# Two transformer blocks in one kernel: projections of the first block and the mixers moved from float32 matmuls to three passes of split operands

## What is computed

```python
h = rms_norm(x, gain)
proj = jnp.einsum('bsd,de->bse', h, w_in)   # q, k, v, g of three branches, q_idx, k_idx, w_idx, f_logit, merge_logit
oa = moba_attention(...) * silu(ga); ob = dsa_attention(...) * silu(gb); oc = forgetting_attention(...) * silu(gc)
y = einsum('nbsw,nwd->bsnd', stack([oa, ob, oc]), w_branch)
merged = jnp.sum(sigmoid(merge_logit).reshape(B, S, N_BRANCH, D_MODEL) * y, axis=2)
x = x + einsum('bsd,de->bse', merged, w_out)
```

```python
h = modulate(rms_norm_2(x, norm), shift, scale)
x = x + 0.5 * g * swiglu(h, w_in, w_out)                       # ffn1, ffn2
x = x + mod[5] * (concatenate([att, conv_or_na]) @ w_out)      # mixer, from pl = h @ w_in
```

## Time and profile before

| | us |
|---|---|
| median of 3 runs (2820.1 to 2823.27) | 2822.03 |
| the profiled execution, time | 2823.07 |
| its span | 2821.3 |
| TensorE matmuls busy | 2710.4 |
| VectorE / ScalarE / GpSimd busy | 1028.1 / 759.1 / 86.3 |
| DMA, mean | 125 GB/s |

### The profile page before, as it was taken

The page is one execution under the profiler, slowest core; times in us unless marked ns, Lnnn a source line. Parts: engine busy times, 40 slices in busy tenths (PEclk is TensorE's granted clock), DMA queues, the critical chain, the costliest instruction groups (busy, mean ns, idle before and its releaser), DMA issues.

```text
span 2821.3 us, 35941 instructions
## 1 busy us (share of the span) xinstructions
PE 2710.4 (96%) x14818; PEld 2130.8 (76%) x14818; DVE 1028.1 (36%) x1672; ACT 759.1 (27%) x1309; POOL 86.3 (3%) x97
## 2 busy tenths in 40 slices
PE   7999999999998999999999899999899999999899
PEld 6877788877886888874455478888688886766899
DVE  0142420142433433330475244333433342045654
ACT  1113311113314222223136242122422223135433
POOL 0000000000000000000380000000000000000000
PEclk9999999999999999999999999999999999999999
DMA  5334444334443232221255232223123222441453
GB/s 218 132 118 149 166 149 163 143 113 158 178 152 132 95 121 77 90 105 64 98 218 191 79 120 89 100 92 121 73 93 114 91 92 90 135 180 47 149 201 112
DMA packets 62656, 353.38 MB, mean 125 GB/s; under 512 B 14384, under 2 KB 17456, under 8 KB 26416
## 3 DMA queue, kind: packets, MB, share of 16 engines
q1 hardware_dynamic: 62512, 351.33, 35.1%
HBM read 350.26 MB, written 1.05 MB: 125 GB/s over the span
## 4 chain that ended last, share of the span: by engine, by line
PE 91%; DVE 5%; ACT 3%; issue 1%; DMA 1%; SPq 0%; ACTq 0%; DVEq 0%
PE psum L655 45%; PE psum L927 15%; PE psum L929 15%; PE psum L928 15%; DVE slab L1797 1%; PE psum L797 1%; ACT slab L1270 1%; DVE stat L1755 1%; DVE w_lo L1809 1%; ACT squares L1248 0%; DMA x<-in_x 0%; DVE squares L1682 0%; ACT slab L1290 0%; DVE psum L1751 0%; DVE slab L1768 0%
## 5 line engine op out<-in xcount | busy, mean ns | idle before, releaser
L655 PE MATMUL psum<-slab,wring 128*128 128x256 f32 (+1 forms) x3460 | 873.9, 413 | 7.0 <-ACT slab L1270 4.4
L655 PEld LDWEIGHTS psum<-slab,wring 128*128 128x128 f32 x3460 | 657.8, 192 | 202.8 <-issue 117.3
L927 PE MATMUL psum<-h_hi,w_hi 128*128 128x512 f32 (+1 forms) x1408 | 516.6, 367 | 21.3 <-DVE h_lo L1678 13.7
L928 PE MATMUL psum<-h_lo,w_hi 128*128 128x512 f32 (+1 forms) x1408 | 515.1, 366 | 0.0
L929 PE MATMUL psum<-h_hi,w_lo 128*128 128x512 f32 (+1 forms) x1408 | 514.9, 366 | 0.0
L1809 DVE TENSOR_TENSOR w_lo<-wring,w_hi 128x1024 fp32r<-128x1024 f32 (+1 forms) x240 | 317.8, 1330 | 330.1 <-ACT w_hi L1364 329.9
L1364 ACT ACTIVATE w_hi<-wring 128x1024 fp32r<-128x1024 f32 (+1 forms) x240 | 272.7, 1142 | 606.7 <-PE psum L929 534.7
L927 PEld LDWEIGHTS psum<-h_hi,w_hi 128*128 128x128 f32 x1408 | 269.1, 191 | 63.6 <-issue 19.2
L928 PEld LDWEIGHTS psum<-h_lo,w_hi 128*128 128x128 f32 x1408 | 269.2, 191 | 41.8
L929 PEld LDWEIGHTS psum<-h_hi,w_lo 128*128 128x128 f32 x1408 | 268.8, 191 | 41.8
L928 PE MATMUL psum<-hidden_lo,w_hi 128*128 128x512 f32 (+1 forms) x704 | 255.6, 363 | 0.0
(11 more groups left out here) (128 smaller groups left out, 1693.1 us busy)
## 6 DMA issues: line engine op xcount, KB each, us to landing
wring<-in_w_b_ffn_in SPq DMA_DIRECT2D x88, 1024.0 KB, 4.8
wring<-in_w_mod SPq DMA_DIRECT2D x72, 1024.0 KB, 4.8
wring<-in_w_b_ffn_out SPq DMA_DIRECT2D x64, 704.0 KB, 4.0
wring<-in_w_b_merge SPq DMA_DIRECT2D x24, 1024.0 KB, 4.8
wring<-in_w_b_out SPq DMA_DIRECT2D x16, 1024.0 KB, 4.8
wring<-in_w_b_in SPq DMA_DIRECT2D x16, 1024.0 KB, 4.9
wring<-in_w_b_q SPq DMA_DIRECT2D x12, 1024.0 KB, 4.8
wring<-in_w_b_k SPq DMA_DIRECT2D x12, 1024.0 KB, 4.8
```

What stands on the lines that cost most here:

```text
L655: return nc.tensor.matmul(out, lhsT, rhs, start=(k == 0), stop=(k == n - 1))
L927: nc.tensor.matmul(acc, wh[:, k, :], rhs_hi[k], start=(k == 0), stop=False)
L928: nc.tensor.matmul(acc, wh[:, k, :], rhs_lo[k], start=False, stop=False)
```

## The change

- All of q, k, v, g and merge of the first block, and b2.0.in, b2.0.out, b2.1.in, b2.1.out, run in three passes (`features3`, `tokens3`). qi, misc, branch and out of the first block, uq, ukv and the modulations stay float32.
- One sequence of weight pieces goes through the kernel (`piece_of`). Of a mixer chunk `w_hi` takes the rounded halves, and the differences are written into the ring slot, over the raw weights (`ring_lo`). A piece is rounded when the piece four before it is multiplied.
- Norms take their weight pieces `ahead`: two between the squares of k=6 and k=7, and two later, in place of the four ahead of all squares. b1 norms and mixer norms make `h_hi` and `h_lo` too. `ffn_weights` goes.
- Mixer outputs are written as hi and lo (a cast and a subtraction), and so is the convolution's (`split_conv`).
- Two modulation chunks move from the convolution to uq, and the convolution's mean, centre, square and variance two steps earlier. Buffers are laid out anew in two areas beside the FFN's parts. The one-hot rows give way to columns of the identity, and their DMA goes.

```diff
-MOD_PLACES = [("b1.0.att", 9), ("b1.1", 2), ("b1.1.att", 11), ("b2.0.n1", 2), ("b2.0.nm", 2), ("b2.0.conv", 5), ("b2.0.uq", 5), ("b2.0.heads", 6),
+MOD_PLACES = [("b1.0.att", 9), ("b1.1", 2), ("b1.1.att", 11), ("b2.0.n1", 2), ("b2.0.nm", 2), ("b2.0.conv", 3), ("b2.0.uq", 7), ("b2.0.heads", 6),
...
-        for at, kind in ((3, "mean"), (4, "center"), (5, "square"), (6, "var"), (12, "root"), (13, "scale"), (14, "silu")):
+        for at, kind in ((1, "mean"), (2, "center"), (3, "square"), (4, "var"), (12, "root"), (13, "scale"), (14, "silu")):
             out[at].append((kind, 0, 0))
+        for at, c in ((12, 0), (13, 1)):
+            out[at].append(("split", 0, c))
+    if nm.startswith("b1"):
+        for c in range(1, 12):
+            out[c].append(("split", l, c))
+    if nm == "b2.1.att":
+        for at, c in ((2, 0), (4, 1)):
+            out[at].append(("split", 1, c))
...
+def split_stage(s):
+
+    return ".ffn" in s or s in ("b2.0.in", "b2.0.out", "b2.1.in", "b2.1.out") or s[0:3] == "b1." and s[5:] in (
+        "merge",) + tuple(f"{part}{br}" for part in "qkvg" for br in range(3))
...
+            def features3(nm, c, rhs, N, tiles, first=0, rotating=None, close=True):
+
+                per = BANK // N
+                lo = mixer_lo(c)
+                for t in range(tiles):
+                    q = piece_of[c] + t
+                    if t % per == 0:
+                        label = f"{nm}.{first + t // per}"
+                        acc = take(label, rotating)
+                    out = acc[:, N * (t % per):N * (t % per) + N]
+
+                    pe.wait_ge(weights_split, q + 1)
+                    for k, (r_hi, r_lo, ready) in enumerate(rhs):
+                        if t == 0 and ready:
+                            if E.new(ready):
+                                pe.wait_ge(*E.at(ready))
+                        nc.tensor.matmul(out, mixer_hi(q)[:, k, :], r_hi, start=(k == 0), stop=False)
+                        nc.tensor.matmul(out, mixer_hi(q)[:, k, :], r_lo, start=False, stop=False)
+                        mm = nc.tensor.matmul(out, lo[:, k, P * t:P * t + P], r_hi, start=False, stop=(k == len(rhs) - 1))
+                    if t == tiles - 1 and close:
+                        E.name_next(f"w{c}")
+                    mm.then_inc(piece_multiplied, 1)
+                    E.step(piece_multiplied, label if t % per == per - 1 or t == tiles - 1 else None)
...
+            def tokens3(nm, c, lhs, halves, toks, first=0, close=True):
+
+                n = P * len(halves)
+                per = BANK // n
+                q = piece_of[c] + halves[0]
+                lo = mixer_lo(c)
+
+                pe.wait_ge(weights_split, piece_of[c] + halves[-1] + 1)
+                for i, t in enumerate(toks):
+                    if i % per == 0:
+                        label = f"{nm}.{first + i // per}"
+                        acc = take(label)
+                    out = acc[:, n * (i % per):n * (i % per) + n]
+                    out2 = out.rearrange("p (a n) -> p a n", n=P)
+                    last = close and i == len(toks) - 1
+                    for k, (l_hi, l_lo, ready) in enumerate(lhs):
+                        if ready:
+                            if E.new(ready):
+                                pe.wait_ge(*E.at(ready))
+                        hi = w_hi[:, q % PARTS:q % PARTS + len(halves), P * k:P * k + P]
+                        nc.tensor.matmul(out2, l_hi[:, P * t:P * t + P], hi, start=(k == 0), stop=False)
+                        mm = nc.tensor.matmul(out2, l_lo[:, P * t:P * t + P], hi, start=False, stop=False)
+                        if last and k == len(lhs) - 1 and len(halves) == 2:
+
+                            mm.then_inc(piece_multiplied, 1)
+                            E.step(piece_multiplied)
+                        mm = nc.tensor.matmul(out, l_hi[:, P * t:P * t + P], lo[:, k, P * halves[0]:P * halves[0] + n],
+                                              start=False, stop=(k == len(lhs) - 1))
+                    if last:
+                        E.name_next(f"w{c}")
+                        mm.then_inc(piece_multiplied, 1)
+                        E.step(piece_multiplied, label)
...
-            def norm(nm):
+            def norm(nm, ahead=None):
 
                 N = NORM_N[nm]
                 for k in range(KD):
+                    if k == KD - 1 and ahead:
+                        for i in range(2):
+                            ahead(i)
...
+            def round_piece(c, i):
+
+                q = piece_of[c] + i
+                act.wait_ge(landed[c % SLOTS], 16 * (c // SLOTS + 1))
+
+                if q >= PARTS:
+                    act.wait_ge(piece_multiplied, q - PARTS + 1)
+                A(mixer_hi(q), slot_of(c).rearrange("p (k n) -> p k n", n=256)[:, :, P * i:P * i + P], ACT.Copy).then_inc(weights_rounded, 1)
+
+            def round_chunk(c):
+                for i in range(2):
+                    round_piece(c, i)
...
-            def modulate(nm, l, which, N):
-
-
+            def modulate(nm, l, which, N, ahead):
+
+
+                if which != 1:
+                    for i in (2, 3):
+                        ahead(i)
                 if E.new(f"{nm}.mscale"):
                     act.wait_ge(*E.at(f"{nm}.mscale"))
                 for k in range(KD):
                     if E.new(f"{nm}.t{k}"):
                         act.wait_ge(*E.at(f"{nm}.t{k}"))
                     for g in range(N // SEQ):
-                        v = (h[:, k, :] if which == 1 else squares[:, k % 4, :])[:, SEQ * g:SEQ * g + SEQ]
-                        last = g == N // SEQ - 1
+                        v = squares[:, k % 4, SEQ * g:SEQ * g + SEQ]
                         A(v, v, ACT.Identity, scale=mscale[:, k, g:g + 1],
                           bias=mods[:, l, 24 * which + k, g:g + 1]).then_inc(shifted, 1)
-                        act.wait_ge(shifted, E.step(shifted, f"{nm}.h{k}" if last and which == 1 else None))
-                    if which != 1:
-                        A(h_hi[:, k, 0:N], squares[:, k % 4, 0:N], ACT.Copy).then_inc(shifted, 1)
-                        act.wait_ge(shifted, E.step(shifted, f"{nm}.hi{k}"))
+                        act.wait_ge(shifted, E.step(shifted))
+                    A(h_hi[:, k, 0:N], squares[:, k % 4, 0:N], ACT.Copy).then_inc(shifted, 1)
+                    act.wait_ge(shifted, E.step(shifted, f"{nm}.hi{k}"))
+                    if which == 1 and k == 3:
+                        for i in (2, 3):
+                            ahead(i)
+
+            def round_plain(nm, ahead):
+                for k in range(KD):
+                    if E.new(f"{nm}.t{k}"):
+                        act.wait_ge(*E.at(f"{nm}.t{k}"))
+                    A(h_hi[:, k, 0:SEQ], h_plain[:, k, :], ACT.Copy).then_inc(shifted, 1)
+                    act.wait_ge(shifted, E.step(shifted, f"{nm}.hi{k}"))
+                    if k == 3:
+                        for i in (2, 3):
+                            ahead(i)
...
+                            n = 8 * br + 2 * "qkvg".index(part) + j
+                            if n not in (14, 15, 23):
+                                round_chunk(flow[n + 2])
...
+                for n in (16, 17):
+                    round_chunk(flow[n])
...
+            def norm(nm, gain=None, to=None, ahead=None, early=True):
 
                 N = NORM_N[nm]
+                if ahead:
+                    for i in range(2):
+                        ahead(i)
...
+                for k in range(KD + 2):
+                    if ahead and k == (2 if early else 6):
+                        for i in (2, 3):
+                            ahead(i)
+                    if k >= 2 and ahead:
+
+                        plain = h_plain[:, k - 2, :] if gain is not None else squares[:, (k - 2) % 4, 0:N]
+                        if E.new(f"{nm}.hi{k - 2}"):
+                            dve.wait_ge(*E.at(f"{nm}.hi{k - 2}"))
+                        V.tensor_tensor(h_lo[:, k - 2, 0:N], plain, h_hi[:, k - 2, 0:N].bitcast(F32), ALU.subtract).then_inc(normed, 1)
+                        dve.wait_ge(normed, E.step(normed, f"{nm}.h{k - 2}"))
...
+            def split_piece(c, i):
+
+                q = piece_of[c] + i
+                raw = slot_of(c).rearrange("p (k n) -> p k n", n=256)[:, :, P * i:P * i + P]
+
+                dve.wait_ge(weights_rounded, q + 1)
+                V.tensor_tensor(mixer_lo(c)[:, :, P * i:P * i + P], raw, mixer_hi(q).bitcast(F32), ALU.subtract).then_inc(weights_split, 1)
+                E.step(weights_split)
+
+            def split_chunk(c):
+                for i in range(2):
+                    split_piece(c, i)
...
-                                V.tensor_copy(u["dst"], o).then_inc(probs_ready, 1)
+                                hi, lo = u["dst"]
+                                V.tensor_copy(hi, o).then_inc(probs_ready, 1)
+                                dve.wait_ge(probs_ready, E.step(probs_ready))
```

(38 more changed lines are left out.)

357 lines of the change are left out of this document (202 added, 155 removed).

## The result

| us | before | changed | ratio (95% interval) |
|---|---|---|---|
| median of four runs | 2822.52 | 2773.06 (2767.72 to 2774.93) | 0.9824 (0.981 to 0.9839) |
| span of the profiled execution | 2821.3 | 2773.1 | |
| mean granted clock of TensorE | 0.978 | 0.967 | |
| sum of TensorE's waits in its timeline | 102.1 | 169.4 | |

What follows compares the result with a forecast made beforehand. TensorE was taken as the bound, 91% of the chain of waits. From 2823.1 us, 132.2 saved on TensorE and 57.0 of longer waits added gave 2747.9, forecast 2748 us, with an 80% range of 2712 to 2785.

Steps and rivals of the forecast that it cites:

- rival 2: First block's attention: 22 steps with a split are paced by the splits, losing 1.3 us each, 29 us, 2777; chance 0.15.
- Gain on TensorE, 132.2: Converted projections: three passes save 97.0 us at N=256 and 38.7 at N=512, less 3.5 lost in b2.1.cv.
- Mix norms, +12 each: b2.0.nm and b2.1.nm: two roundings before the last square, then h_lo at 1.93 us a k; 24 us lost together.
- Norms of the first block, +7: b1.0 and b1.1: 2.0 us of rounding before the last square, then h_lo with two subtractions among them; 14 us lost together.
- Index products, +5.1: Each first-block layer: VectorE's splits of chunks 16 and 17 stand ahead of the RoPE TensorE waits for; 10.2 us lost together.
- Convolution -3, FFN norms -3.7: Second block: two modulation chunks fill the convolution wait; b2.0.n2 -6.3, b2.1.n1 -0.4, b2.0.n1 and b2.1.n2 +1.5 each.
- Behind it top-k shares VectorE with seven splits: hidden.: First block, behind the index products: top-k and splits take 2.0 + 2.4 us per 5.75 us; no loss charged.
- In the attentions of the first block ... nothing charged.: Steps of about 10 us, VectorE and ScalarE idle over half, merge chunk split a step ahead; no loss charged.
- b2.1's attention, +6.5, last nv chunk, +2: b2.1: four subtractions and 4.1 us of rounding lengthen the attention; the last nv chunk's split comes about 2 us late.
- Rival 3: All 84 chunks of N=256: conversion becomes the bound once its chain reaches 7.6 us; at 9.7, 166 us lost, 2914; chance 0.05.
- rival 4: Passes miss the FFN's rate because ring operands are strided; at 0.144 us nothing is saved at N=256, 2845; chance 0.03.
- rival 1: New waits are mostly covered by idle time or other pieces: half of the 57.0 us goes, 2719; chance 0.15.

Runs made afterwards that it cites:

- the first experiment: Changed kernel with the two early roundings before square 4 instead of square 7, in every norm but b1.0's: span 2758.6 us, 14.5 less.

## Why the prediction came out as it did

The mechanism and the sign were right, the range held, and the losses were sized too low: 26.8 us of the forecast gain stayed away. The range was wide enough for that, since it had been drawn to reach over rival 2, whose 2777 lies nearer to the 2773 measured than the 2748 forecast. That nearness is chance: only 9.5 us of the loss come from rival 2's place. The prediction's own sign of being wrong did show, TensorE waiting for `ring_lo` in the merge steps: 11 waits, 10.7 us. Step by step:

- *Gain on TensorE, 132.2.* Right. 0.355 a product at N=256, where 0.359 was taken, gives some 5 us more over 1344 products (an estimate from the 5.68 us a chunk), and N=512 gives 3 to 5 us less, as the ring was assumed to read like `w_lo`. That the two cancel is luck. cv came as taken.
- *Mix norms, +12 each.* First tile at T+30.8 where T+29.3 was worked out, and the second 6.9 and 6.6 us later instead of 5.4, its first passes at the lower clock: +13.7 and +13.4. The last k of the first tile came at T+29.0 (28.7 forecast), so the pace was right; allowing 1 us for the clock was too little. That two roundings lie on the chain is shown by the first experiment, to half a us.
- *Norms of the first block, +7.* In b1.0 the first bank is copied 7.3 us later than before in place of 5.9 net: 1.4 too low.
- *Index products, +5.1.* 6.7 and 5.1 measured, and the cause is shown.
- *Convolution -3, FFN norms -3.7.* The wait fell from 4.09 to 1.29 us; b2.0.n2 -6.1 for -6.3. b2.1.n1 was 1.3 too good.
- *"Behind it top-k shares VectorE with seven splits: hidden."* This step failed. It counted busy time (2.0 + 2.4 in 5.75 us) and not the queue: the last of the seven waits for a rounding that waits 5.59 us for a DMA, and with it everything behind it on both engines; the larger part of the delay ran through ScalarE's queue, which the step does not name. The wait grew by 3.0 and 1.9 us.
- *"In the attentions of the first block ... nothing charged."* This failed too: 9.5 of the 27.6 us due in the merges stayed away. It was rival 2 at a third of its 29 us: the rounding ran a step ahead as said, but behind an instruction that waits for TensorE. The "idle for more than half" was true (VectorE 44% busy, ScalarE 39% between 245 and 355 us of the kernel before) and no help.
- *b2.1's attention, +6.5, last nv chunk, +2.* 9.5 and 5.3. The two terms of the 6.5 add up to 6.0; the one for the chunks (4.1) was too low, as they cost 6.6. (For nv: 2478.4 to 2518.7 was 40.3 us and is 43.3, with 2.3 us of gain in it.) The weights' landing, rounding and subtraction follow each other in full before the last nv chunk; TensorE waits 3.9 us, and its first passes behind that run at the lower clock (0.56 from 2450.7 to 2453.0).
- Rival 3's point was never reached (chunks come every 5.68 us), rival 4 holds only for N=512 and at 3%, and of rival 1 nothing was seen.

## What to carry to other kernels

A conversion of operands costs less by its busy time than by its place in an in-order queue: put each piece of it where its inputs are surely there and ahead of the instruction that waits for TensorE, not behind it. In this kernel moving such work, with no operation removed, was worth another 49 us; that count includes the forget gate's logarithm, which is no conversion and whose 4.7 us of wait a layer stood there before the change too. And where a norm feeds a matmul slowly, give TensorE several output tiles per step: it fills the pauses, and it brings the clock back.

## What was not expected

- The granted clock stays at 0.50 for 19 us while TensorE makes three passes per 1.93 us, with a pause after each three, though it is busy 15.2 of them by the profile; with twelve passes a k and no pause it is 0.50 for the first 3.6 us and 1.00 from there on.
- Passes of N=512 whose third operand lies in the ring start 0.233 us apart, and 0.227 without it; at N=256 passes from the ring start 0.118 to 0.120 apart, those of the FFN 0.120.
- Two chunks' conversion among b2.1's softmax steps costs more than its time on either engine (4.0 us on ScalarE, 4.7 on VectorE): moving it out gave 6.8 us.
